# Three reorderings in a hybrid streaming encoder: k's heads normalised before q's, an embedding transposed in the first down block, a state update moved

## The reference

```python
for i in range(DEPTH):                      # DEPTH = 2
    x = x + 0.5 * swiglu(rmsnorm(x, norm_g[i, 0]), ffn_w_gu[i, 0], ffn_w_d[i, 0])
    xn = rmsnorm(x, norm_g[i, 1])
    y, st = even_mixer(...) if i % 2 == 0 else odd_mixer(...)
    x = x + y
    x = x + 0.5 * swiglu(rmsnorm(x, norm_g[i, 2]), ffn_w_gu[i, 1], ffn_w_d[i, 1])
    xg = rmsnorm(x, norm_g[i, 3])
    x = x + (p[i] @ w_ple[i]) * jax.nn.sigmoid(xg @ w_ple_gate[i])
```

## Time and profile before

| what | value |
|---|---|
| median of three executions | 2698.7 us |
| the profiled execution | 2701.65 us, its span 2699.9 us |
| TensorE busy | 2658.3 us, 98% of the span |
| VectorE / ScalarE / GpSimd busy | 1863.3 / 1068.7 / 529.4 us |
| mean granted TensorE clock | 0.993 of full speed |

### The profile page before, as it was taken

The page is one execution under the profiler, slowest core; times in us unless marked ns, Lnnn a source line. Parts: engine busy times, 40 slices in busy tenths (PEclk is TensorE's granted clock), DMA queues, the critical chain, the costliest instruction groups (busy, mean ns, idle before and its releaser), DMA issues.

```text
span 2699.9 us, 43696 instructions
## 1 busy us (share of the span) xinstructions
PE 2658.3 (98%) x18213; PEld 2619.9 (97%) x18213; DVE 1863.3 (69%) x2179; ACT 1068.7 (40%) x1558; POOL 529.4 (20%) x251
## 2 busy tenths in 40 slices
PE   9999999999999999999999999999999999999998
PEld 9999999999998799999999999999999999999998
DVE  7748386987677778476577974848666786584756
ACT  5425253243222545344345552524411254252545
POOL 2130303332010030302113202030333311102041
PEclk9999999999999899999999999999999999999999
DMA  4222223232003222223232232232222223232231
GB/s 134 83 73 85 79 75 90 58 78 55 17 9 87 75 67 79 79 78 94 64 90 69 82 91 71 81 92 75 85 79 77 63 79 94 63 96 66 82 101 50
DMA packets 401149, 205.57 MB, mean 76 GB/s; under 512 B 15555, under 2 KB 398940, under 8 KB 400953
## 3 DMA queue, kind: packets, MB, share of 16 engines
q1 hardware_dynamic: 400746, 202.70, 26.4%
q10 hardware_dynamic: 206, 0.08, 0.0%
HBM read 195.14 MB, written 7.60 MB: 75 GB/s over the span
## 4 chain that ended last, share of the span: by engine, by line
PE 55%; DVE 8%; ACT 1%; issue 1%; POOL 0%; DVEq 0%; ACTq 0%
PE ps L928 9%; PE ps L929 9%; PE ps L930 9%; PE ps L913 9%; PE ps L917 9%; PE ps L914 9%; DVE ut L2203 1%; DVE x L2937 1%; DVE sumsq L2302 1%; DVE r L2388 1%; DVE hf L2810 1%; DVE x L3123 0%; PE ps L1203 0%; DVE wlo L2219 0%; DVE hl L2291 0%
## 5 line engine op out<-in xcount | busy, mean ns | idle before, releaser
L861 POOL TENSOR_TENSOR wlo<-raw,whi 128x1024 fp32r<-128x1024 f32 (+2 forms) x214 | 518.0, 2424 | 2131.4 <-ACT whi L1632 2131.2
L913 PE MATMUL ps<-xh,whi 128*128 128x320 f32 x1552 | 472.3, 312 | 7.9 <-POOL wlo L861 5.7
L914 PE MATMUL ps<-xl,whi 128*128 128x320 f32 x1552 | 467.2, 309 | 0.0
L913 PE MATMUL ps<-hh,whi 128*128 128x320 f32 x1440 | 437.7, 312 | 4.1 <-POOL wlo L861 1.8
L914 PE MATMUL ps<-hl,whi 128*128 128x320 f32 x1440 | 435.0, 310 | 0.0
L928 PE MATMUL ps<-tau_hi,whi 128*128 128x320 f32 x1280 | 396.4, 310 | 2.9 <-DVE wlo L2219 2.0
L930 PE MATMUL ps<-tau_hi,wlo 128*128 128x320 f32 x1280 | 395.5, 309 | 0.0
L929 PE MATMUL ps<-tau_lo,whi 128*128 128x320 f32 x1280 | 395.5, 309 | 0.0
L1632 ACT CAST whi<-raw 128x1024 fp32r<-128x1024 f32 (+2 forms) x216 | 208.3, 966 | 390.9 <-PE ps L917 352.0
L917 PE MATMUL ps<-xh,wlo 128*128 128x320 f32 x1552 | 353.6, 309 | 0.0
L917 PE MATMUL ps<-hh,wlo 128*128 128x320 f32 x1440 | 329.1, 310 | 0.0
(11 more groups left out here) (434 smaller groups left out, 4817.0 us busy)
## 6 DMA issues: line engine op xcount, KB each, us to landing
raw<-in_ffn_w_gu SPq DMA_DIRECT2D x320, 256.0 KB, 3.8
raw<-in_ffn_w_d SPq DMA_DIRECT2D x64, 512.0 KB, 4.0
raw<-in_w_in_even SPq DMA_DIRECT2D x32, 512.0 KB, 4.0
raw<-in_ffn_w_d SPq DMA_DIRECT2D x32, 384.0 KB, 3.6
raw<-in_w_in_odd SPq DMA_DIRECT2D x24, 512.0 KB, 3.7
raw<-in_ffn_w_gu SPq DMA_DIRECT2D x16, 512.0 KB, 4.5
raw<-in_w_ple_gate SPq DMA_DIRECT2D x16, 512.0 KB, 3.9
raw<-in_w_out_even SPq DMA_DIRECT2D x8, 512.0 KB, 4.2
```

Of the source, the lines that this page charges most:

```text
L861: pool.tensor_tensor(ring(wlo, n), raw[:, slot, 0:kt, :], ring(whi, n).bitcast(fp32), ALU.subtract).then_inc(lo_ready, 1)
L913: pe.matmul(ps[j % 4][:, c, 0:HT], wh[:, k], hi[:, k, cs], start=(k == 0), stop=False)
L914: pe.matmul(ps[j % 4][:, c, 0:HT], wh[:, k], lo[:, k, cs], start=False, stop=False)
```

## The change

It does three things and adds or removes no instruction.

1. `norm_head` turns the order of the head norms, so that k's heads come first and q's last. With all k heads ready by b = 10, the head of tile 0 is taken out of "core": TensorE makes the token rows of tile 0 in the middle of plain block 11 (their transpose goes to bank 6 instead of 4), VectorE makes gcols and W(1) before it takes block 11 (`delta_scales`), and W(0) and v before the last head norm (`delta_rows`). In tile 0 the filling of 24 is split in 12 before `kk` and 12 before `np`, which now waits for the last head norm.
2. In the last "down" stage of f = 1, of both layers, the two pT jobs are made before block 0's job, and their transposes take the place of the two row blocks of block 1 as filling. VectorE makes the high and low parts of p before it takes block 0.
3. In the sample tile `keep_state` goes from behind level 1 to behind level 3. TensorE waits for it (`core["up"]`) in the middle of the state products, before head 2.

The diff, without some lines of context:

```diff
+        def norm_head(q):
+            return (q + HA) % (2 * HA)
...
                 s = dict(kind="down", n0=len(blocks), kt=cnt, last=last, scale=-0.5, hbase=first_pair + j0, layer=i, tau=None, hid=other(prod - 1),
                          prod=prod if last else None, g=(i * 4 + (1 if f == 0 else 3)) * KD)
+                if last and f == 1:
+                    s["pT"] = [job("pT") for _ in range(KP)]
                 for o in range(KD):
                     blk((dn, o * P, j0 * P), cnt, "down")
-                    if last and f == 1 and o == 1:
-                        s["pT"] = [job("pT") for _ in range(KP)]
...
-                pe.transpose(bank(4)[:, 0:P], R1[:, tile(t)], ident[:]).then_inc(core["bcast"], 1)
+                pe.transpose(bank(4 if t else 6)[:, 0:P], R1[:, tile(t)], ident[:]).then_inc(core["bcast"], 1)
...
-                if t == 0:
-                    token_rows(0)
-                z_fill(s, filled, 24)
+                z_fill(s, filled, 24 if t else 12)
                 pe.wait_ge(core["prod"], t + 1)
                 per_head(4, lambda h: k[:, h], lambda h: W(0)[:, h]).then_inc(core["kk"], 1)
                 if t:
                     pe.wait_ge(core["up"], t)
-                per_head(3, lambda h: k[:, h], lambda h: q[:, h]).then_inc(core["np"], 1)
-                mlstm_part(t, "gates")
+                    per_head(3, lambda h: k[:, h], lambda h: q[:, h]).then_inc(core["np"], 1)
+                    mlstm_part(t, "gates")
+                else:
+                    mlstm_part(t, "gates")
+                    z_fill(s, filled, 12)
+                    pe.wait_ge(hn_used, s["even"]["hn0"] + 2 * HA)
+                    per_head(3, lambda h: k[:, h], lambda h: q[:, h]).then_inc(core["np"], 1)
...
                     if h == HA // 2:
                         sample_part("vt")
+                        pe.wait_ge(core["up"], t)
...
                         if late and o == 0:
                             mm(s["n0"], *s["hid"], first=hidden, part=(0, kt - 1))
-                            mm(s["n0"] + 1, *s["hid"], part=(0, 2))
+                            if "pT" in s:
+                                pe.wait_ge(p_loaded, 32 * (s["layer"] + 1))
+                                for q, j in enumerate(s["pT"]):
+                                    tposes(j, [(t // 4, t % 4 * P, pstage[:, t, q * P:(q + 1) * P]) for t in range(NTILE)])
+                            else:
+                                mm(s["n0"] + 1, *s["hid"], part=(0, 2))
                             mm(s["n0"], *s["hid"], first=hidden, part=(kt - 1, kt))
-                        elif late and o == 1:
+                        elif late and o == 1 and "pT" not in s:
...
-                        mm(n + NA + 1 + b, *s["side"])
+                        if b < NA - 1:
+                            mm(n + NA + 1 + b, *s["side"])
+                        else:
+                            mm(n + NA + 1 + b, *s["side"], part=(0, KD // 2))
+                            pe.wait_ge(rows_ready, 1)
+                            for c in (0, 3):
+                                pe.wait_ge(slot_free[c], (s["jobs"] + 3 - c) // 4)
+                            token_rows(0)
+                            mm(n + NA + 1 + b, *s["side"], part=(KD // 2, KD))
...
-                pe.wait_ge(rows_ready, 1)
...
-                            head_squares(s, q, s["l2"], qkv[:, q, :])
+                            head_squares(s, q, s["l2"], qkv[:, norm_head(q), :])
...
-                keep_state(t - 1, gcol)
...
                 own(dve.tensor_tensor(W(7), W(7), heads(1), ALU.subtract).then_inc(core["xr"], 1), core["xr"])
+                keep_state(t - 1, gcol)
                 mul(W(5), heads(5), W(5))
...
                 elif kind == "down":
+                    for q, j in enumerate(s.get("pT", [])):
+                        done(j)
...
+                        free(j)
                     for o in range(KD):
...
                     for b in range(NA):
+                        if b == NA - 1:
+                            dve.wait_ge(out_stored, 4 * 16)
+                            delta_scales(0)
                         j = block_job[n + NA + 1 + b]
                         done(j)
...
                         if q >= 0:
-                            head_norm(s, q, qkv[:, q, :], float(DK) ** -0.5 if q < HA else 1.0)
+                            if b == NA - 1:
+                                delta_rows(0)
+                            head = norm_head(q)
+                            head_norm(s, q, qkv[:, head, :], float(DK) ** -0.5 if head < HA else 1.0)
```

More of the change, by code:

```diff
@@ L476, in stream_step @@
                     s["l2"].append(job("hn"))
+        s["jobs"] = len(jobs)
         stages.append(s)
         Z_ORDER = [0, 1, 2, 4, 3, 5, 6, 7]
-        stages.append(dict(kind="core", jobs=len(jobs), z0=len(blocks), side=side(prod - 1)))
+        stages.append(dict(kind="core", jobs=len(jobs), even=s, z0=len(blocks), side=side(prod - 1)))
         for q in Z_ORDER:
@@ L1545, in _ @@
                             mm(s["n0"] + o, *s["hid"], first=hidden if o == 0 else None)
-                        if o == 1 and "pT" in s:
-                            pe.wait_ge(p_loaded, 32 * (s["layer"] + 1))
-                            for q, j in enumerate(s["pT"]):
-                                tposes(j, [(t // 4, t % 4 * P, pstage[:, t, q * P:(q + 1) * P]) for t in range(NTILE)])
                 elif kind == "even_in":
@@ L2408, in masked, with delta_scales @@
                 own(dve.tensor_tensor(W(1), W(4), over_heads(level[:, l, :]), ALU.mult).then_inc(core["ctl"], 1), core["ctl"])
[L2410 to L2412 removed]
+            def delta_scales(t):
                 dve.wait_ge(core["bcast"], t + 1)
[L2415 removed]
+                o1(dve.tensor_copy(gcols[:], bank(4 if t else 6)[:, 32:32 + GC]))
                 for h in range(HA):
@@ L2952, in _ @@
                         pair_ahead(s["n0"] + o)
-                        if o == 1 and "pT" in s:
-                            for q, j in enumerate(s["pT"]):
-                                done(j)
-                                for c, z in ((0, slice(0, SEQ)), (1, slice(SEQ, T))):
-                                    w = z.stop - z.start
-                                    high, low = s["hid"]
-                                    o1(dve.tensor_copy(high[:, PH + q, z], ps[j % 4][:, c, 0:w]))
-                                    sm = h_ready if c else dve_own
-                                    own(dve.tensor_tensor(low[:, PH + q, z], ps[j % 4][:, c, 0:w], high[:, PH + q, z].bitcast(fp32),
-                                                          ALU.subtract).then_inc(sm, 1), sm)
-                                free(j)
                 elif kind == "even_in":
```

18 lines of the change are left out of this document (13 added, 5 removed).

## The result

| | median us | lowest, highest | executions |
|---|---|---|---|
| before | 2700.24 | 2697.48, 2703.16 | 20 |
| changed | 2705.94 | 2699.29, 2709.87 | 20 |

What follows compares the result with a forecast made beforehand. TensorE, busy 98% of the span, was taken to bound the kernel. The terms -0.85 - 0.65 + 5.8 - 3.2 + 3.0 gave +4.1 us, so 2698.7 + 4.1 = 2702.8 us (+0.15%), range 2696.5 to 2707.5.

Steps and rivals of the forecast that it cites:

- Stall, 2.9 us in each layer: Last down stage: block 0 waits until VectorE has read the last pair's X; 2.9 us per layer, 5.8 in all.
- Given back, 3.2: Down blocks after the stall: TensorE's waits for GpSimd go or shrink in both layers, 3.2 us back, between 0 and 3.4.
- Part one, 0.85: Join of "even_in" and "core", tile 0: transposes begin at 656.9 instead of 657.75, gain 0.85 us, bounds 0 and 1.9.
- 0.3 later as now: Join, tile 0: VectorE takes block 11 0.3 us after its end at 647.1, as before the change, until 648.2.
- Part two, 0.65: Sample tile: without the state update between levels 1 and 2, TensorE's 0.66 wait goes; gain 0.65 us, bounds 0 and 1.5.
- the -1.5 of the forecast: Join and sample tile: forecast gains of parts one and two, -0.85 and -0.65 us.
- The clock, 1.5 for each stall: Behind block 0's stall in each layer: a fall of TensorE's clock costing 1.5 us, +3.0 for two places.
- the first rival: Last down stage: the clock holds at both stalls, same sum without the 3.0, 2699.8 us; chance 0.27.
- The second rival: Last down stage: no stall, slot free when block 0 begins; only the gains stand, 2695.2 us; chance 0.07.
- The fourth: Slower than before: stalls bring clock falls of 10.2 us, 5.1 us each, 2710.0; chance 0.18, shared with little given back.

Runs made afterwards that it cites:

- part three alone: Kernel before with only the pT jobs and transposes moved ahead of block 0 of the last down stage: 2703.36 us (+3.3), ratio 1.0014.
- the renumbered part three: Kernel before with the p transposes moved, but their jobs numbered after block 0's, with a semaphore for p: 2698.39 us (-2.0), ratio 0.9992.
- part two alone: Kernel before with only the sample tile's state update moved behind level 3: 2702.66 us (+0.6), ratio 1.0003.
- part one alone: Kernel before with only k's heads first and the head of tile 0 taken into block 11: 2699.76 us (-1.5), ratio 0.9996.
- Parts one and two together: Changed kernel with the pT jobs and p's transposes put back where they were: 2699.03 us (-2.0), ratio 0.9991.
- the filled stall: Changed kernel with 24 products whose result nobody reads put in TensorE's wait before block 0: 2702.12 us (+0.3), ratio 1.0002.
- the renumbered kernel: Changed kernel with the pT jobs numbered after block 0's, a semaphore for p, instruction order kept: 2696.49 us (-4.5), ratio 0.9981.
- the slot alone: Kernel before with only the pT jobs numbered ahead of block 0, a semaphore for p, no instruction moved: 2727.13 us (+24.5), ratio 1.0093.
- the half-filled state products: Renumbered pT jobs in the changed kernel, plus 16 unread 128-column products, behind every second narrow state product: 2700.43 us (-2.2), ratio 0.9994.

## Why the prediction was right

The sign, the size (+4.3 by the ratio, between 2.7 and 5.9, against +4.1) and the mechanism held: the slot of the last pair's X, the stall, the clock behind it, and less given back than lost. That the two numbers agree to 0.2 us is luck: the terms as measured below add up to between +5.2 and +6.1. Step by step:

- **Stall, 2.9 us in each layer.** Shown: block 0 is 2.85 us late in both, ended by the sum that reads X. Renumbering the jobs alone removed it.
- **Given back, 3.2.** Shown, as waiting time: 3.0 in the changed kernel, 3.0 with part three alone, none without it. The executions agree where no stall is mixed in: -2.0 us for the renumbered part three, between -4.6 and +0.3.
- **Part one, 0.85.** Smaller. VectorE takes block 11 at 647.87, 0.65 us behind the start of the sums (647.22), where I had "0.3 later as now" (645.46 against 645.19). All that comes after moves by that. The first wait of the sample tile that both timelines show (861.83 before, 861.42 changed) is 0.41 us earlier. The profiles don't enter this stretch at one time: the kernel with part two alone, which has it unchanged, is at its sums at 645.32 where the kernel before is at 645.19, and the changed kernel shares that delay (the sums of an earlier head, the same in both, start at 604.79 where they started at 604.66), so some 0.55 us are gained. The profile of part one alone gives the same: its wait stands at 861.51, and its sums of that earlier head at 604.88. What makes VectorE take the block later I did not find.
- **Part two, 0.65.** 0.60 by the timelines, the wait of 0.66 is gone as said, and no wait came in its place. Parts one and two together timed at -2.0 (0.9991), between -4.9 and -0.3, which the -1.15 of the timelines and the -1.5 of the forecast both fit.
- **The clock, 1.5 for each stall.** This is the term whose parts were mis-sized, in two ways that nearly cancel. A fall as in the changed kernel's profile costs 2.7 us up to the transposes (7.23 against 4.51), near twice my price. But it doesn't seem to come each time: the changed kernel's executions lie in groups at 2699.3 to 2700.2, 2702.8 to 2703.9, 2705.9 to 2706.1 and 2708.8 to 2709.9 (3, 5, 8 and 4 of them), some 3 us apart, with mean clocks from 0.995 down to 0.990. That these steps are falls, at the stalls or in the sample tile, is argued from their size. The profiles of three kernels show three outcomes at a stall of 2.69 us: no low stretch, one of 3.4 us and one of some 6.7, each time alike in both layers. For the changed kernel itself there is an estimate: a mean clock of 0.995 in its fastest execution leaves some 27 us at the lower level in all (24 to 30 with the rounding). Two falls of 6.7 us and the 7 to 10 us that every profile has in its tail would leave at most 9 of them for the sample tile, where no profile without added products has under 23. So the falls most likely didn't come there. On average the changed kernel paid 4.5 us for the clock by the filled stall (3.8 by the ratios) and 3.6 by the renumbered kernel, where I had 3.0; the scatter is too large to tell these from 3.0.

The rule that the clock holds unless idle gaps are longer than these stalls (the Trainium skill, TensorE: Matmul & The Clock Gate, "Why this matters for your kernels") would have given 2699.8 us and was the first rival. It fell: with 2.69 us of idle time the clock went down in the changed kernel's profile at both places, and filling the gap took 4.5 us off. The clock did stay up in the profile of part three alone, so the rule describes some executions. The second rival (no stall) fell with the waits of 2.69 us. The fourth, falls as long as 10.2 us, didn't come: they were 6.7 us long.

One sum doesn't close well. Part three alone timed at +3.3 and parts one and two at -2.0, together +1.3, where the change had +4.8. With the same 5.7 less 3.0 in it, the clock would have cost part three alone 0.6 us and the whole change 4.1. The three intervals leave room for it. Whether parts one and two make the falls more frequent, by shifting the time at which the stalls come, stays open; no run tests it.

## What to carry to other kernels

Where buffers rotate by job number, moving a step also moves the buffers of its neighbours: write down for each job of the stretch who held its slot before and when that is read out, before and after the move. The number and the place in time can be chosen apart, and here that turned +4.8 us into -4.5. And where a wait can't be avoided on TensorE between dense stretches, products whose result nobody reads, put into it, can be cheaper than idle time (here +0.3 against +4.8 us).

## What the runs showed of the hardware

- With a stall of 2.69 us between dense stretches TensorE was at 1.2 GHz for some 6.7 us in one profile (1396.4 to 1403.1) and for 3.4 us in another (1397.1 to 1400.5, the slot alone), and stayed at 2.4 GHz in a third (part three alone); a wait of 1.38 us, and that of 1.69 of the earlier trace rows, left it up where they were seen.
- Being busy by the profile's count is not enough. In a stretch made up mostly of products of 32 columns TensorE was busy for 15.84 of 16 us from 872 to 888 and had a granted clock of 0.54. With one product of 128 columns behind each of the narrow ones it was 1.00 there, and the kernel's time came out some 2.6 us lower than without them (-7.1 against -4.5, ratios 0.9973 and 0.9981, each on its own chip, so this difference alone is not beyond the scatter; the clock and the 13.2 us that became 9.4 are seen directly).
- The changed kernel's twenty times lie in four groups about 3 us apart, and the half-filled state products gave two groups some 6 us apart, so a median of three can't show an edit of 3 us.
